# Expert rows entered in pieces of one token tile over a ring of up to eighteen slots, and the matrix-memory weights computed one head ahead

## What is computed

```
# matrix memory, per head, both directions d, against 256 context and 256 own tokens
w      = exp(log_weight[d] - row_max)
y[d]   = (q @ k.T * w) @ v / max(|sum(q @ k.T * w)|, exp(-m))
m      = rms(y[0] + y[1]) * norm_g * sigmoid(o)
merged = (sigmoid(g_m) * (m @ w_bm) + sigmoid(g_a) * (a @ w_ba)) @ w_out
# experts, per token, 8 heads
s1, i1 = top_k(q1 @ keys1, 16);  s2, i2 = top_k(q2 @ keys2, 16)
top, pos = top_k(all 256 sums of s1 and s2, 16);  idx = i1[..] * 128 + i2[..]
act = gelu(sum(expert_u[idx] * x));  out = sum(softmax(top) * act * expert_v[idx])
```

## Time and profile before

| | us |
|---|---|
| median of 3 runs | 1433.34 |
| lowest, highest | 1432.47, 1435.71 |
| the profiled execution | 1433.3 |
| its span, first to last instruction | 1431.5 |
| PE busy | 1221.5 (85%) |
| DVE busy | 831.9 (58%) |
| ACT busy | 283.4 (20%) |
| POOL busy | 310.2 (22%) |
| DMA, mean over the span | 269 GB/s |

### The profile page before, as it was taken

The page is one execution under the profiler, slowest core; times in us unless marked ns, Lnnn a source line. Parts: engine busy times, 40 slices in busy tenths (PEclk is TensorE's granted clock), DMA queues, the critical chain, the costliest instruction groups (busy, mean ns, idle before and its releaser), DMA issues.

```text
span 1431.5 us, 13992 instructions
## 1 busy us (share of the span) xinstructions
PE 1221.5 (85%) x4976; PEld 735.7 (51%) x4976; DVE 831.9 (58%) x2117; ACT 283.4 (20%) x872; POOL 310.2 (22%) x278
## 2 busy tenths in 40 slices
PE   7998899989989979986978999787776598777786
PEld 5876568766845757753447555333322243333332
DVE  2635635555433568654254667767676767676654
ACT  1113300142210233221021222111111121111111
POOL 0000000000000010000012446544354264444530
PEclk9999799999999999998988999999999799999998
DMA  8551135722245344620337999999999899999995
GB/s 345 211 227 66 53 118 186 302 75 67 111 176 190 142 174 177 243 81 0 118 133 314 390 421 420 420 421 421 419 421 421 357 420 421 421 420 421 420 421 216
DMA packets 48853, 385.69 MB, mean 269 GB/s; under 512 B 5648, under 2 KB 7440, under 8 KB 9104
## 3 DMA queue, kind: packets, MB, share of 16 engines
q0 software_dynamic: 36864, 268.45, 45.5%
q1 hardware_dynamic: 11920, 116.35, 21.4%
HBM read 383.73 MB, written 1.05 MB: 269 GB/s over the span
## 4 chain that ended last, share of the span: by engine, by line
PE 57%; DMA 28%; DVE 8%; ACT 4%; issue 2%; POOL 2%; SPq 0%; DVEq 0%; POOLq 0%; ACTq 0%
DMA arena<-peer_uv_in,arena 25%; PE bank L468 21%; PE bank L474 15%; PE bank L1033 12%; DMA wring<-peer_uv_in,arena 2%; PE bank L509 2%; DMA wring<-w_in 1%; DVE arena L1446 1%; PE bank L699 1%; DVE arena L2061 1%; DVE arena L1454 1%; POOL arena L2141 1%; PE bank L612 1%; ACT arena L1113 1%; PE bank L541 1%
## 5 line engine op out<-in xcount | busy, mean ns | idle before, releaser
L1033 PE MATMUL bank<-arena 128*128 128x512 f32 x480 | 229.2, 621 | 49.5 <-DVE arena L1446 25.7
L1033 PE MATMUL bank<-wring,arena 128*128 128x512 f32 x368 | 193.0, 667 | 78.8 <-ACT arena L1424 78.8
L474 PE MATMUL bank<-hT,wring 128*128 128x256 f32 (+1 forms) x1152 | 221.9, 355 | 4.3 <-issue 2.2
L474 PEld LDWEIGHTS bank<-hT,wring 128*128 128x128 f32 x1152 | 195.1, 198 | 32.6 <-issue 10.5
L468 PE MATMUL bank<-wring,hT 128*128 128x256 f32 (+2 forms) x656 | 196.7, 458 | 9.5 <-DMA wring<-w_in 5.3
L2061 DVE CUSTOM_DVE_ANT_0 arena<-arena 128x1024 f32<-128x1024 f32 x120 | 147.2, 1228 | 91.8 <-DMA arena<-peer_uv_in,arena 91.7
L1033 PEld LDWEIGHTS bank<-arena 128*128 128x128 f32 x480 | 95.6, 202 | 176.5 <-issue 145.6
L2117 POOL TENSOR_TENSOR small<-small,const 128x1 f32<-128x1 f32 (+3 forms) x18 | 16.1, 895 | 730.5 <-DVEq L1458 598.7
L2141 POOL DMA_INDIRECT arena<-peer_uv_in,arena x120 | 141.6, 1180 | 141.8 <-PE bank L1033 133.3
L1033 PEld LDWEIGHTS bank<-wring,arena 128*128 128x128 f32 x368 | 72.5, 205 | 183.4 <-ACT arena L1424 106.5
L468 PEld LDWEIGHTS bank<-wring,hT 128*128 128x128 f32 x656 | 124.7, 193 | 73.1 <-issue 55.5
(11 more groups left out here) (197 smaller groups left out, 1150.8 us busy)
## 6 DMA issues: line engine op xcount, KB each, us to landing
wring<-w_in SPq DMA_DIRECT2D x22, 2048.0 KB, 8.2
wring<-ada_in SPq DMA_DIRECT2D x12, 2048.0 KB, 8.1
wring<-wo_in SPq DMA_DIRECT2D x6, 2048.0 KB, 8.1
wring<-pq_in SPq DMA_DIRECT2D x4, 2048.0 KB, 8.8
wring<-cmp_in SPq DMA_DIRECT2D x2, 2048.0 KB, 8.9
wring<-br_in SPq DMA_DIRECT2D x2, 2048.0 KB, 10.1
wring<-w1b_in SPq DMA_DIRECT2D x2, 1120.0 KB, 8.5
wring<-w_in SPq DMA_DIRECT2D x2, 1024.0 KB, 8.8
```

What stands on the lines that cost most here:

```text
L474: ins = pe.matmul(bank[:, at:at + n_tok], w[:, k, col:col + P], rhs[:, k, :], start=(k == 0), stop=(k == KC - 1))
L1033: ins = pe.matmul(sums_of[half][:, :], diag[:, at % NDIAG, :], v_row[slot_of[at]][:, half * 512:(half + 1) * 512], start=(n == 0), stop=(n ...
```

## The change

**Matrix memory.** `dw` gets a second copy (half of `hT`), and so do `negmu`, `flo_in` and `flo_e`. The maxima of head 0 move into the last attention rounds on DVE, those of head h + 2 stand behind head h, and ACT's exponentials run one head ahead. PE transposes an item, does another piece (`between`), and then multiplies it with the values. Normalising starts with tile 0 while item 7 is under way; "bm", the merge and "gT" go by tile. The load of the expert keys `sk` waits for the matrix memory's last sum, since it fills a half that `dw` now borrows.

**Expert entry.** Queries are made for one tile at a time. Before row 0 PE makes chunks 0 and 1 for tile 0 and chunk 0 for tile 1; the other 20 pieces of 128 tokens follow one by one at fixed rows up to 61, key scores between them and up to row 69. There are 18 slots: nine at row 0 (two of them new, in the masks' constants and in tile 1's scores), two more at rows 24, 50 and 76, three at 86; the slot in tile 1's scores is given back at row 50. Groups are of two rows for the first 96 rows, then of four, at the end 2, 1, 1. The table `choice_at` says at which row DVE does which step of `choose`: half of head 1's steps now stand ahead of row 0, the rest beside rows 0 to 7. POOL computes the inverse root of tile 1 between the third and the fourth gather. The sums of tile 1 use two rotating banks. The result of a tile goes out in two halves.

```diff
-SLOTS = 16
+SLOTS = 18
...
-        new_slots = {0: [0, 1, 2, 6, 3, 4, 5]}
-        for row, c in ((7, 1), (25, 2), (43, 3)):
+        sizes = [2] * 48 + [4] * ((ROWS - 100) // 4) + [2, 1, 1]
+        LAST_EARLY = 17
+        new_slots = {0: [0, 1, 2, 6, 16, 17, 3, 4, 5]}
+        for row, c in ((24, 1), (50, 2), (76, 3)):
...
-        new_slots[57] = [13, 14, 15]
+        new_slots[86] = [13, 14, 15]
...
+        choice_at = {-1: [(1, n) for n in range(8)]}
+        for n in range(8):
+            choice_at[n] = [(1, 8 + n)]
+        for h in range(2, TT * EH):
+            first_row = 8 + 14 * (h - 2) if h < 6 else 16 * (h - 2)
...
             for h in range(MH):
-                if h + 1 < MH:
-                    key_rows(h + 1)
                 for t in range(TT):
                     i = TT * h + t
+                    mlstm_transposes(i)
+                    if t == 0 and h + 2 < MH:
+                        key_rows(h + 2)
+                    between(i + 1)
                     mlstm_values(i)
-                if h + 1 < MH:
-                    mlstm_scores(h + 1)
+                    if t == 0 and h + 1 < MH:
+                        mlstm_scores(h + 1)
...
-                sums_of = [job(("pv", t, half), "acc") for half in range(2)]
+                sums_of = [job(("pv", t, half), "rot" if t else "acc") for half in range(2)]
...
-                if chunk == ("br", 0, 0):
-                    full(sp, ("akv", 1))
+                if chunk == ("wo2", 0, 0):
+                    full(sp, ("mo", 1))
...
+                if h == 0:
+                    row_maxima(1)
+                    attn_out(1)
...
+                if h + 2 < MH:
+                    row_maxima(h + 2)
...
             for head in range(TT * EH):
...
                     here = slot_of[at]
+                    if at == 3:
+                        root(1)
```

More of the change, by code:

```diff
@@ L1098, in _ @@
             for t in range(TT):
-                sp.wait_ge(sem("result"), t + 1)
-                sp.dma_start(out[t * P:(t + 1) * P, :], x3[:, t, :]).then_inc(sem("stored"), 16)
-            sp.wait_ge(sem("stored"), 16 * TT)
+                for half in range(2):
+                    c = slice(half * 512, (half + 1) * 512)
+                    sp.wait_ge(sem("result"), 2 * t + half + 1)
+                    sp.dma_start(out[t * P:(t + 1) * P, c], x3[:, t, c]).then_inc(sem("stored"), 16)
+            sp.wait_ge(sem("stored"), 16 * 2 * TT)
         @block.scalar
@@ L1383, in choice_exp, with rows_back @@
                                accum_out=esum[:, e + 1:e + 2]).then_inc(sem("top_exp"), 1)
[L1385 to L1387 removed]
+            def rows_back(t):
                 for half in range(2):
@@ new lines, in _ @@
+            for g, size in enumerate(sizes):
+                two = slice((g % 2) * GROUP, (g % 2) * GROUP + size)
+                at = starts[g]
+                col = at % (2 * TOPK)
+                act.wait_ge(sem("dots"), at + size)
+                act.activation(g_sq[:, two], dots[:, col:col + size], ACT.Square, scale=GELU_SQ).then_inc(sem("gelu_sq"), 1)
+                act.wait_ge(sem("gelu_in"), g + 1)
+                act.activation(g_tanh[:, two], g_in[:, two], ACT.Tanh).then_inc(sem("gelu_tanh"), 1)
+                act.wait_ge(sem("w_ready"), g + 1)
+                for r in range(size):
+                    if at + r >= NDIAG:
+                        act.wait_ge(sem("row_used"), at + r + 1 - NDIAG)
+                    w = (g % 4) * GROUP + r
+                    act.activation(diag[:, (at + r) % NDIAG, :], ident, ACT.Copy, scale=wcur[:, w:w + 1]).then_inc(sem("diag_ready"), 1)
+                if g == 0:
+                    for b in range(4):
+                        queries(0, b, 1)
+                for piece in filler(g - 1) if g else []:
+                    if piece[0] == "q":
+                        queries(*piece[1:])
+                    elif piece[0] == "h2":
+                        rows_back(1)
+                    else:
+                        if piece == ("ps", 1, 0):
+                            act.wait_ge(sem("row_used"), last_score + 1)
+                        key_scores(*piece[1:])
+                for row in range(at, at + size):
+                    if row in exp_after:
+                        choice_exp(exp_after[row])
@@ new lines, in _, with merge @@
+            latent(0)
+            branch_a(3)
+            latent(1)
+            def merge(half, t):
+                c = slice(half * 512, (half + 1) * 512)
+                bank = full(dve, ("bm", half, t))
+                free(stt(rt_b, gates[:, half * 4 + t, :], 1.0, bank[:, :], ALU.add, ALU.mult), ("bm", half, t))
+                taken(dve, ("bm", half, t))
+                link(tt(mrg[:, t, c], mrg[:, t, c], rt_b, ALU.add), "mrg")
+            merge(0, 0)
+            merge(1, 0)
+            merge(0, 1)
@@ L2099, in _ @@
             out_rows(1, 1)
-            rms_rows(h2, 1, sumsq[:, 1:2], 6)
-            for part in range(16):
-                choose(1, part)
             for half in range(2):
```

405 lines of the change are left out of this document (221 added, 184 removed).

## The result

The changed kernel takes 1392.4 us (median of 4 runs, 1391.1 to 1394.9) against 1433.0 us of the kernel before beside it: ratio 0.9715, 95% interval 0.9696 to 0.9733. The profiled execution has a span of 1391.1 us, 40.4 us less than the earlier trace rows; the prediction had 41.6.

What follows compares the result with a forecast made beforehand. Row part bound by DMA bytes at 420 GB/s; gains of 21.1 (front), 0.3 (start), 9.7 (entry), 5.4 (tile change) and 5.1 (tail) sum to 41.6 us, giving 1391.7 us; eight-in-ten range 1383 to 1406.

Steps and rivals of the forecast that it cites:

- What bounds the kernel: Row part: bound by bytes, 256 rows of 1.05 MB at 420 GB/s, 639 us, whatever the engines do.
- Matrix memory: Front, 77.2 us stretch: 12.4 us idle less about 1, plus 3.5 from PE's clock; 14.9 us gained.
- Normalising and branches: After the last values: 4.4 us in place of 9.6, 5.2 gained; "bm" to second "wo2" by tile, 1 us.
- Start and entry: Stream's start: gathers 3.6 us earlier, net 0.3 us; entry holes of 14.7 us cut to 5, 9.7 us gained.
- Change of tiles: Between tile 0's and tile 1's sums: rotating banks end PE's wait, and 5.4 us come back.
- the stream only moves: Rival: holes are made good elsewhere, so only front and start count; 1412 us, chance 5%.
- Tail: After the last dot product: groups 2, 1, 1 leave only the last row, 1.2 us for 6.3; 5.1 us gained.
- Half the front: Rival in the matrix memory: the new order makes PE wait elsewhere, 12 of 21 us stay lost; 1404 us, chance 12%.
- The starved ring: Rival: with nine to twelve slots until row 76, a turn takes 25 us, not 17; 1404 or 1408 us, chance 12%.
- Pairs too dear for DVE: Rival, slower than before: each pair pays its own DVE-ACT round trip; at 6.0 us a pair 1440 us, chance 4%.

Runs made afterwards that it cites:

- the repeat: The changed kernel run once more with no edit, against the kernel before: 1389.1 us, ratio 0.9688 (0.9672 to 0.9705).

## Why the prediction was right, and where not

**What bounds the kernel: right, with one limit missing.** It called the row part bound by bytes at 420 GB/s. All kernels with a full stream lie at 656.9 to 657.2 us, except the two that changed how many packets of DVE's program fall into it. So the limit is the bytes of the busiest of the sixteen engines, which also carries DVE's program: 1 us for each 8 KB packet of it.

**Matrix memory: mechanism right, size low.** 14.9 us predicted, 19.5 measured. The idle time fell by 11.7 us (12.4 to 0.7), as the step said (12.4 - 1). The clock's share was mis-sized: I took 3.5 of 7 us; PE's busy time fell by 7.9 us (64.8 to 57.0), since the granted clock was 1.00 throughout. This was the upper bound of the term. That it was 1.00 is in part luck of this trace. In the repeat PE idles as little (0.7 us), yet from 609.7 us on its matmuls ran at 1.2 GHz for 3.4 us with no idle time ahead of them, and the same stretch took 59.5 us. So the prediction's step from "no longer idles" to "the clock stays up" holds for most of the 14 us at the lower level and not for all.

**Normalising and branches.** 5.1 us against 5.2. The 1.0 us from "bm" to "wo2" did not come: 32.9 us as before, at a granted clock of 0.94. The 2.1 us by which attention ended later stood in no term; they are there already where PE does the same attention scores (577.4 us before, 579.4 now), ahead of the first piece that moved on PE, and lie within the scatter of the front.

**Start and entry: the gain was right by two errors.** First, no hole was left, where I had left 5 us as a ring of nine slots had run at 391 GB/s. Row 0 on PE was forecast at 761 us on the old clock, and came at 739.9 + 22.5 = 762.4; the tenth gather at 764, and came at 764.6. The 391 GB/s belonged to nine to eleven slots with groups of four and PE's old order; the run with seven slots and fours shows that kind of loss, and either remedy ends it. The bound that left 1 us lost was the near one. Second, the prediction summed holes as if each were worth its length. The lone engine's lag was 4.0 us before (1412.6, from the table of that kernel's end, to 1416.64) and is 9.5 us now (1368.7 to 1378.24): fewer holes, fewer chances to catch up. The holes that went are 20.1 us and the first gather's earlier start behind the indices 3.4 (0.3 us behind them and not 3.7); less 5.5 us of lag that is 18.0, and 15.9 were measured. The missing 2.1 us may be query bytes now inside the stream, for which the prediction had 3.3; that was not measured apart.

**Change of tiles: the step that failed.** 5.4 us were forecast. The hole is gone on the page and PE's wait too, but undoing this edit alone costs nothing (657.1 and 657.1 us). The rival "the stream only moves" was right at this one place. Its mechanism was another than the one I gave: not later stretches make the hole good, but one engine during it. My argument against it, that nothing is lost from 1140 us on, looked at the mean of sixteen engines, and that mean can't show it.

**Tail: size wrong.** 5.1 us predicted, 2.0 measured (3.4 in the repeat; 0.4 to 3.5 over the ten traces with these last groups, by where PE's clock is low). "Only the last row is left" overlooked what PE has queued: it gets rows 248 to 251 at 1370.99 us and is busy with eight rows to the end. Pairs in front of the last rows made it 9.5 us, the 9.8 that were forecast.
The half store took 1391.1 - 1388.48 = 2.6 us, where I had kept the 3.05 of the row of the whole one. (The 3.2 beside it in the prediction was not that row's; so the half store saved 0.4 us and not 0.6.) The Trainium skill (DMA: Bandwidth & Descriptors, Anatomy of one DMA) gave 2.6 for it, as an estimate, by its sum of 2.0 us and the bytes at 436 GB/s; this trace agrees with it.

**The rivals.** Half the front: did not happen, PE waits 0.7 us in the matrix memory. The starved ring: not in the change, but real once both remedies are undone. Pairs too dear for DVE: no, with pairs DVE waits for DMA, not DMA for DVE, and fours are no faster.

## What to carry to other kernels

A stream of DMAs ends with its slowest engine: look at the DMA share behind the mean stream's end (0.06 is one of sixteen), and do not sum holes that are shorter than that engine's lag. Where a transfer loop starves, ring depth and group size are two remedies for one thing; try each alone before adding both. Ahead of the last small groups leave no large one: what counts is what PE has queued when the last input lands.

## What the runs showed of the hardware that was not expected

- DVE's program comes by 8 KB packets of queue q14 through the DMA engine that here is the slowest. Each took 0.33 us in the packet records, but set this engine's gathers back by 0.9 to 1.0 us. 696 more DVE instructions brought six packets and 6.0 us, which is 116 instructions a packet; two packets less brought 2.2 us less.
- PE's program comes by 16 KB packets of queue q8 (eight more for 2088 more instructions, 657.2 us) and ACT's by q14 too (five more, 656.9 us); neither delayed the end. With ACT's code the second latest engine was 5.0 us late at the last gather in place of 2.7, so ACT's program goes by an engine other than DVE's. Why isn't settled. The Trainium skill (DMA: Bandwidth & Descriptors, Queues, rings and completion order) says that row 14 of the DMA queues is the runtime's, for refills among others, and that an engine takes turns between its queues by packets. The first agrees with the 30 packets on q14, if that is the row that the profile calls q14; why a turn costs three times its packet's duration, no run here shows.
- The front of kernels whose front is the same scatters by up to 7 us between executions. Up to 4 us of it are there at PE's hundredth matmul (30.3 to 34.4 us), ahead of any stretch at the lower clock. Part of the rest goes with PE's clock: its two levels stand at other places in each trace, and ahead of the first gather the lower one adds up to 71 to 75 us. What sets either was not tried.
